# Decoder step: the down projection of the ConvFFN's full groups in five matmuls a block in place of six

## What is computed

```python
def conv_ffn(hn, w_up, w_fconv, w_down, prefix):
    up = hn @ w_up                              # 2048 -> 2 x 5504
    up_c, state = causal_dwconv(up, prefix, w_fconv)
    g, u = jnp.split(up_c, 2, axis=-1)
    return (jax.nn.silu(g) * u) @ w_down, state # 5504 -> 2048
...
ffn, ffn_st = conv_ffn(rms_norm(x, norm_ffn), w_up, w_fconv, w_down, ffn_prefix)
x = x + ffn
```

## Time and profile before

| | us |
|---|---|
| median of three runs | 2513.88 |
| lowest and highest of them | 2513.48, 2515.24 |
| the profiled execution, its own time | 2513.66 |
| span of that execution, first to last instruction | 2512.1 |
| mean granted TensorE clock, share of full speed | 0.995 |

### The profile page before, as it was taken

The page is one execution under the profiler, slowest core; times in us unless marked ns, Lnnn a source line. Parts: engine busy times, 40 slices in busy tenths (PEclk is TensorE's granted clock), DMA queues, the critical chain, the costliest instruction groups (busy, mean ns, idle before and its releaser), DMA issues.

```text
span 2512.1 us, 45839 instructions
## 1 busy us (share of the span) xinstructions
PE 2484.5 (99%) x19827; PEld 2461.3 (98%) x19827; DVE 1214.0 (48%) x2028; ACT 636.3 (25%) x857; POOL 128.7 (5%) x158
## 2 busy tenths in 40 slices
PE   9999999999999999999999999999999999999997
PEld 8999999999999999999999999999999999999996
DVE  6824554547323556553355434554355534544346
ACT  7422222223223352222122211222122211222123
POOL 0010101000111030000000000000000000000004
PEclk9999999999999999999999999999999999999999
DMA  7332323242622332232222222222223222232223
GB/s 286 110 115 84 109 86 107 82 127 62 230 94 85 135 82 85 85 100 86 85 85 90 96 85 85 90 91 89 85 85 97 80 94 83 87 99 85 94 77 117
DMA packets 69722, 252.73 MB, mean 101 GB/s; under 512 B 8504, under 2 KB 12936, under 8 KB 68256
## 3 DMA queue, kind: packets, MB, share of 16 engines
q1 hardware_dynamic: 64144, 224.16, 27.6%
q0 software_dynamic: 5248, 25.71, 3.0%
q10 hardware_dynamic: 144, 0.05, 0.0%
HBM read 240.80 MB, written 9.09 MB: 99 GB/s over the span
## 4 chain that ended last, share of the span: by engine, by line
PE 94%; DVE 3%; DMA 1%; POOL 1%; issue 1%; ACT 0%; SPq 0%; DVEq 0%; POOLq 0%; ACTq 0%
PE ps_out L979 89%; POOL sq_sum L640 1%; DVE x_t L1895 1%; PE ps_out L1035 0%; PE ps_out L1037 0%; PE ps_out L1036 0%; DVE w_lo L1383 0%; DMA out_conv_s<-pe 0%; DVE a_lo L1389 0%; DMA w_raw<-in_wall 0%; PE ps_out L1238 0%; DMA x_t<-in_x 0%; PE ps_b L1044 0%; PE ps_out L1271 0%; DVE x_t L1904 0%
## 5 line engine op out<-in xcount | busy, mean ns | idle before, releaser
L979 PE MATMUL ps_out<-a_hi,w_hi 128*128 128x272 f32 x4704 | 978.2, 290 | 3.2 <-DVE w_lo L1383 3.2
L979 PE MATMUL ps_out<-a_lo,w_hi 128*128 128x272 f32 x4704 | 975.2, 289 | 0.0
L979 PE MATMUL ps_out<-a_hi,w_lo 128*128 128x272 f32 x4704 | 975.0, 289 | 0.0
L979 PEld LDWEIGHTS ps_out<-a_hi,w_hi 128*128 128x128 f32 x4704 | 738.5, 189 | 7.6 <-issue 6.6
L979 PEld LDWEIGHTS ps_out<-a_lo,w_hi 128*128 128x128 f32 x4704 | 738.5, 188 | 0.0
L979 PEld LDWEIGHTS ps_out<-a_hi,w_lo 128*128 128x128 f32 x4704 | 738.1, 188 | 0.0
L662 ACT ACTIVATE w_hi<-w_raw 128x1024 fp32r<-128x1024 f32 x402 | 410.9, 1050 | 695.9 <-PE ps_out L979 679.5
L1383 DVE TENSOR_TENSOR w_lo<-w_raw,w_hi 128x1024 fp32r<-128x1024 f32 x402 | 481.6, 1229 | 133.9 <-ACT w_hi L662 130.0
L1418 DVE TENSOR_TENSOR x_t<-ps_out,x_t 128x544 f32<-128x544 f32 x112 | 81.1, 724 | 414.9 <-PE ps_out L979 402.2
L979 PE MATMUL ps_out<-h_hi,w_hi 128*128 128x272 f32 x1280 | 265.3, 289 | 0.4
L979 PE MATMUL ps_out<-h_lo,w_hi 128*128 128x272 f32 x1280 | 264.9, 288 | 0.0
(11 more groups left out here) (356 smaller groups left out, 1524.4 us busy)
## 6 DMA issues: line engine op xcount, KB each, us to landing
w_raw<-in_wall SPq DMA_DIRECT2D x406, 512.0 KB, 3.8
x_t<-in_x SPq DMA_DIRECT2D x4, 1088.0 KB, 9.3
x_t<-in_x POOLq DMA_DIRECT2D x4, 1088.0 KB, 10.2
kc_t<-in_k_cache POOLq DMA_DIRECT2D x1, 4096.0 KB, 24.0
vc_t<-in_v_cache POOLq DMA_DIRECT2D x1, 4096.0 KB, 13.8
out_y<-x_t SPq DMA_DIRECT2D x7, 544.0 KB, 3.0
rows<-gate_rows POOLq DMA_DIRECT2D x4, 816.0 KB, 7.2
c_smp<-in_c_smp POOLq DMA_DIRECT2D x4, 512.0 KB, 7.7
```

What stands on the lines that cost most here:

```text
L979: ins_ = nc.tensor.matmul(out_bank(o, k)[:, 0:n[1]][:, ::-1], w, a[:, c, m:m + n[1]][:, ::-1], start=first and t == 0, stop=last and t == 2)
```

## The change

The eight chunks' high and low parts, which lay in two tiles of 544 columns a chunk, lie in one tile `h_seg` of 1088 columns a chunk, cut in three segments: the first 272 high columns and the first 92 low ones (`LA`) of the one half, the same of the other half, and the remaining 180 low columns of both halves (`LB`). With the high weight TensorE multiplies the three segments, 364, 364 and 360 columns, into the two banks of the output and one bank of `ps_a`. With the low weight it multiplies the two high parts, 272 columns each, into the first 272 columns of the output's banks (`five`). The waits and the two counts of `half_used` a unit stay where they were. In the banks, the low terms of a half now lie in two places beside the rest, so VectorE's addition to `x_t` becomes three (`add_five`): the `ps_a` bank, the last 92 columns of the output's banks, and the old one, which waits for the second. ScalarE writes the high part in three copies, VectorE the low part in four subtractions. The rest of three chunks keeps the old layout (`plain`).

```diff
--- before.py
+++ after.py
@@ -199,6 +199,12 @@
         kc_t = at("kc_t", R_Y, [P, H, NB, NM])
         h_hi = at("h_hi", R_Y, [P, GRP, T], F32R)
         h_lo = at("h_lo", R_Y + GRP * T * 4, [P, GRP, T], F32R)
+        LA = 92
+        LB = TH - LA
+        h_seg = at("h_seg", R_Y, [P, GRP, 2 * T], F32R)
+        hs_hi = h_seg[:, :, 0:2 * (TH + LA)].rearrange("p c (a t) -> p c a t", a=2)[:, :, :, 0:TH]
+        hs_la = h_seg[:, :, 0:2 * (TH + LA)].rearrange("p c (a t) -> p c a t", a=2)[:, :, :, TH:TH + LA]
+        hs_lb = h_seg[:, :, 2 * (TH + LA):2 * T].rearrange("p c (a t) -> p c a t", a=2)
         l_hi = at("l_hi", R_AH, [P, LDN_UNITS - RING, UB * P], F32R)
         l_lo = at("l_lo", R_AL, [P, LDN_UNITS - RING, UB * P], F32R)
         w_raw = at("w_raw", R_RAW, [P, RING, UB * P])
@@ -903,7 +909,7 @@
             split_hi(Index(U_FFN + 3))
 
 
-            def hidden(u0, j, c, first):
+            def hidden(u0, j, c, first, plain=False):
 
                 if not (first and j == 0):
                     splits(u0 + 4 * j)
@@ -913,8 +919,14 @@
                 nc.scalar.activation(cv[0][:, 0:CEXT - 2], cv[0][:, 0:CEXT - 2], ACT.Silu).then_inc(g_silu, 1)
                 splits(u0 + 4 * j + 2)
                 act.wait_ge(h_prod, (c + 1).value())
-                nc.scalar.activation(h_hi[:, j, 0:SEQ], cv[0][:, 0:SEQ], ACT.Copy).then_inc(h_hi_done, 1)
-                nc.scalar.activation(by_smp(h_hi[:, j, SEQ:T]), smp(cv[0], 2)[:, :, 0:NT], ACT.Copy).then_inc(h_hi_done, 1)
+                if plain:
+                    nc.scalar.activation(h_hi[:, j, 0:SEQ], cv[0][:, 0:SEQ], ACT.Copy).then_inc(h_hi_done, 1)
+                    nc.scalar.activation(by_smp(h_hi[:, j, SEQ:T]), smp(cv[0], 2)[:, :, 0:NT], ACT.Copy).then_inc(h_hi_done, 1)
+                else:
+                    nc.scalar.activation(hs_hi[:, j, 0, :], cv[0][:, 0:TH], ACT.Copy)
+                    nc.scalar.activation(hs_hi[:, j, 1, 0:SEQ - TH], cv[0][:, TH:SEQ], ACT.Copy).then_inc(h_hi_done, 1)
+                    nc.scalar.activation(by_smp(hs_hi[:, j, 1, SEQ - TH:TH]), smp(cv[0], 2)[:, :, 0:NT],
+                                         ACT.Copy).then_inc(h_hi_done, 1)
 
             def group(u0, c0, first=False):
                 for j in range(GRP):
@@ -926,7 +938,7 @@
             for g in range(1, NG):
                 group(Index(U_FFN + g * FU), Index(g * GRP))
             for j in range(REST):
-                hidden(Index(U_LAST), j, Index(NG * GRP + j), False)
+                hidden(Index(U_LAST), j, Index(NG * GRP + j), False, plain=True)
 
             def final_root(n):
                 act.wait_ge(ssq, S_FIN + n + 1)
@@ -1300,25 +1312,43 @@
                     pe.wait_ge(h_lo_done, (c0 + c + 1).times(2).value())
                 return wait
 
+            def five(o, u, chunks, marks, wait=None, late=False):
+
+                s = u.mod(RING)
+                pe.wait_ge(hi_ready, (u + 1).value())
+                pe.wait_ge(lo_ready, (u + 1).value())
+                seg = TH + LA
+                places = [(out_bank(o, 0), 0, seg), (out_bank(o, 1), seg, 2 * seg), (ps_a[:, o.mod(2), :], 2 * seg, 2 * T)]
+                for c in chunks:
+                    if wait is not None:
+                        wait(c)
+                    wh, wl = w_hi[:, s, P * c:P * c + P], w_lo[:, s, P * c:P * c + P]
+                    for n, (bank, a, z) in enumerate(places):
+                        m = nc.tensor.matmul(bank[:, 0:z - a][:, ::-1], wh, h_seg[:, c, a:z][:, ::-1], start=c == 0,
+                                             stop=n == 2 and c == GRP - 1, skip_group_check=True)
+                    if late:
+                        m.then_inc(half_used, 1)
+                    for bank, a, z in places[0:2]:
+                        m = nc.tensor.matmul(bank[:, 0:TH][:, ::-1], wl, h_seg[:, c, a:a + TH][:, ::-1], start=False,
+                                             stop=c == GRP - 1, skip_group_check=True)
+                    if c in marks:
+                        m.then_inc(half_used, 1)
+
             def down2(o, u, wait):
 
                 for m in range(2):
                     free(o + m)
-                    blocks(o + m, u + m, [(b, b, b == 0, False, m == 0 and b == 3) for b in range(GRP - 1)],
-                           h_hi, h_lo, (2, TH), wait if m == 0 else None)
+                    five(o + m, u + m, range(GRP - 1), (3,) if m == 0 else (), wait if m == 0 else None)
                 for m in range(2):
 
-                    blocks(o + m, u + m, [(GRP - 1, GRP - 1, False, True, True)], h_hi, h_lo, (2, TH),
-                           wait if m == 0 else None, late=m == 1)
-
+                    five(o + m, u + m, [GRP - 1], (GRP - 1,), wait if m == 0 else None, late=m == 1)
             def group(u0, o0, c0, first=0):
                 for j in range(first, 2 * GRP):
                     output(o0 + j, u0 + 2 * j, a_hi, a_lo)
                 down2(o0 + 2 * GRP, u0 + 4 * GRP, hidden_waits(c0))
                 for m in range(2, KD):
                     free(o0 + 2 * GRP + m)
-                    blocks(o0 + 2 * GRP + m, u0 + 4 * GRP + m, [(b, b, b == 0, b == GRP - 1, b % 4 == 3) for b in range(GRP)],
-                           h_hi, h_lo, (2, TH))
+                    five(o0 + 2 * GRP + m, u0 + 4 * GRP + m, range(GRP), (3, GRP - 1))
 
             group(Index(U_FFN), Index(O_FFN), Index(0), first=1)
             for g in range(1, NG):
@@ -1416,6 +1446,15 @@
             def add_to_x(o, m):
 
                 tt(halves(x_t[:, m, :]), out_view(o), halves(x_t[:, m, :]), ALU.add).then_inc(evacuated, 1)
+
+            def add_five(o, m):
+
+                x = halves(x_t[:, m, :])
+                own = ps_out[:, 2 * o.mod(2):2 * o.mod(2) + 2, :]
+                rest = ps_a[:, o.mod(2), 0:2 * LB].rearrange("p (a t) -> p a t", a=2)
+                tt(x[:, :, LA:TH], rest, x[:, :, LA:TH], ALU.add)
+                link(tt(x[:, :, 0:LA], own[:, :, TH:TH + LA], x[:, :, 0:LA], ALU.add))
+                tt(x, out_view(o), x, ALU.add).then_inc(evacuated, 1)
 
             def conv3(dst, src, taps):
 
@@ -1846,7 +1885,7 @@
             for e in ext:
                 link(nc.vector.memset(e[:, 0:2], 0.0))
 
-            def hidden(u0, o0, j, c, first):
+            def hidden(u0, o0, j, c, first, plain=False):
 
                 for k in range(2):
                     n = (c.times(2) + k).value()
@@ -1867,9 +1906,18 @@
                 dve.wait_ge(g_silu, (c + 1).value())
                 tt(cv[0][:, 0:CEXT - 2], cv[0][:, 0:CEXT - 2], cv[1][:, 0:CEXT - 2], ALU.mult).then_inc(h_prod, 1)
                 dve.wait_ge(h_hi_done, (c + 1).times(2).value())
-                tt(h_lo[:, j, 0:SEQ], cv[0][:, 0:SEQ], h_hi[:, j, 0:SEQ], ALU.subtract).then_inc(h_lo_done, 1)
-                tt(by_smp(h_lo[:, j, SEQ:T]), smp(cv[0], 2)[:, :, 0:NT], by_smp(h_hi[:, j, SEQ:T]), ALU.subtract)\
-                    .then_inc(h_lo_done, 1)
+                if plain:
+                    tt(h_lo[:, j, 0:SEQ], cv[0][:, 0:SEQ], h_hi[:, j, 0:SEQ], ALU.subtract).then_inc(h_lo_done, 1)
+                    tt(by_smp(h_lo[:, j, SEQ:T]), smp(cv[0], 2)[:, :, 0:NT], by_smp(h_hi[:, j, SEQ:T]), ALU.subtract)\
+                        .then_inc(h_lo_done, 1)
+                else:
+                    tt(hs_la[:, j, :, :], cv[0][:, 0:2 * TH].rearrange("p (a t) -> p a t", a=2)[:, :, 0:LA],
+                       hs_hi[:, j, :, 0:LA], ALU.subtract)
+                    tt(hs_lb[:, j, 0, :], cv[0][:, LA:TH], hs_hi[:, j, 0, LA:TH], ALU.subtract)
+                    tt(hs_lb[:, j, 1, 0:SEQ - TH - LA], cv[0][:, TH + LA:SEQ], hs_hi[:, j, 1, LA:SEQ - TH],
+                       ALU.subtract).then_inc(h_lo_done, 1)
+                    tt(by_smp(hs_lb[:, j, 1, SEQ - TH - LA:LB]), smp(cv[0], 2)[:, :, 0:NT],
+                       by_smp(hs_hi[:, j, 1, SEQ - TH:TH]), ALU.subtract).then_inc(h_lo_done, 1)
 
             def group(u0, o0, c0, first=False):
                 for j in range(GRP):
@@ -1877,13 +1925,13 @@
                 for m in range(KD):
                     splits(u0 + (4 * GRP + m), 1)
                     summed(u0 + (4 * GRP + m))
-                    add_to_x(o0 + (2 * GRP + m), m)
+                    add_five(o0 + (2 * GRP + m), m)
 
             group(Index(U_FFN), Index(O_FFN), Index(0), first=True)
             for g in range(1, NG):
                 group(Index(U_FFN + g * FU), Index(O_FFN + g * FO), Index(g * GRP))
             for j in range(REST):
-                hidden(Index(U_LAST), Index(O_LAST), j, Index(NG * GRP + j), False)
+                hidden(Index(U_LAST), Index(O_LAST), j, Index(NG * GRP + j), False, plain=True)
 
             def final_scale(n):
                 dve.wait_ge(root, S_FIN + n + 1)
```

## The result

| | us |
|---|---|
| before, median of 15 runs | 2514.80 (2511.85 to 2516.21) |
| changed, median of 15 runs | 2520.29 (2517.83 to 2523.76) |
| ratio | 1.0024, 95% interval 1.0017 to 1.0032 |
| changed, the profiled execution, its time and its span | 2520.72, 2519.2 |

The changed kernel is slower by 4 to 8 us, where 3 us less was forecast and the range ended at 2518.5. The page shows what was meant to happen: 640 matmuls fewer than in the earlier trace rows, and the work of VectorE grown by 68 us. But the span grew.

The account below looks back on a forecast made before the run. TensorE's unbroken matmuls were taken to bound the kernel: -7.43 us for fewer matmuls and +4.15 us for the additions gave -3.3 us, stated as 2510.6 us; own range 2508.8 to 2512.6, widened to 2508.5 to 2518.5.

Parts of the forecast that it names:

- What bounds the kernel: ConvFFN: one unbroken stretch of matmuls per group, 287.54 us for 2298, plus one VectorE addition of 0.74 us a group.
- A fixed 11.7 ns for each matmul instruction, whatever its width: Down outputs: one matmul fewer in each of 640 blocks saves 11.7 ns each, 7.49 us in all.
- The ends of that term: Matmul saving: either the fixed part vanishes on three wide matmuls, 22.5 us more saved, or nothing is saved.
- One that grows with the columns (nothing saved): Down matmuls: overhead is a share of the columns, nothing saved, +4.15 us, 2518.0 us; rival's chance 0.05.
- The pieces of 16 columns: Down matmuls: operand fetched in whole 16-column pieces, three more a block, 20 ns, +9.5 us in sum, 2523.4; chance 0.12.
- The three additions: VectorE's addition to x: 1.55 us in place of 0.72, seen once in each of five groups, +4.15 us.
- What stays hidden: ScalarE's extra copies and VectorE's extra subtractions: last low half at most 0.6 us later, under 3.8 us of cover.
- The clock: Longer TensorE stops, some 1.05 us, lower the granted clock: +4.1 us, 2518.0 us; rival's chance 0.05.
- Slower: Whole kernel above 2518.9 us: chance 0.14, from the 16-column pieces (0.12) and 0.02 of the two rivals at 2518.

Follow-up runs that it names:

- noflip: The changed kernel with the five matmuls of a block reading and writing their columns in ascending, not descending, order: 2512.10 us in a single run, 740.2 ns a block.
- la88_noflip: The changed kernel in ascending order with LA = 88 in place of 92, a single run: 740.4 ns a block.
- la96: The changed kernel with LA = 96 in place of 92, all segments on multiples of 16 columns: 2522.25 us against 2514.22 before, ratio 1.0030.
- la94: The changed kernel with LA = 94 in place of 92, segments starting at columns 0, 366 and 732, a single run: 753.4 ns a block.
- dve3: The kernel before with three VectorE operations in place of each one addition of a down output: 2518.20 us, ratio 1.0017.
- before_cover: The kernel before with blocks reordered so that three, not one, cover a group's first addition: 2511.68 us against 2514.06, ratio 0.9991.
- readflip: The changed kernel reading operands in descending order as it does but writing PSUM in ascending order, a single run: 752.1 ns a block on average.
- best_w32: The kernel of noflip_cover with the split weights 32 bytes further on in SBUF: 2519.45 us against 2514.78 before, ratio 1.0018.
- wshift: The changed kernel, descending, with the split weights and all behind them 64 bytes further on in SBUF: 2526.86 us, single run, beside 2516.84 before.
- best_w128: The kernel of noflip_cover with the split weights 128 bytes further on in SBUF: 2512.07 us against 2514.78 before, ratio 0.9989.
- la94_noflip: The changed kernel in ascending order with LA = 94 in place of 92, a single run: 740.0 to 750.0 ns a block, differing by group.
- before_noflip: The kernel before with the matmuls of line 979 reading and writing in ascending order: 2519.52 us against 2514.07, ratio 1.0022.
- zero_h: The changed kernel with the high and low operands of the full groups set to zero: 2523.75 us in a single run.
- psoff: The changed kernel, descending, with the third segment's 360 columns at the end of their PSUM bank, a single run: 289.58 us a group.
- noflip_cover: The changed kernel with its five matmuls ascending and three blocks covering a group's first addition: 2507.11 us against 2514.07 before, ratio 0.9969.

## Why the prediction was wrong

- **What bounds the kernel.** Right. The loss lies in the two places that were named, the matmuls of the down outputs and the one addition on the chain. Nothing else in the stage waits.
- **A fixed 11.7 ns for each matmul instruction, whatever its width.** This is the step that failed. It rested on two widths, 256 and 272 columns, 6% apart, and was carried to 364, and on rows of one order and one placement. One argument for it carried nothing, that the loss doesn't come with a change of weights: the earlier trace rows has as many weight loads as matmuls, 19827 each, so every matmul brings a load whether its weights change or not. Over the 680 ns that 1632 columns stream, a block of six loses 70 ns, one of five 73.3 in the changed kernel, and 60 to 73.4 over all cuts, orders and placements tried. In the best of them (740.0 ns) it is 12.0 ns an instruction, in the changed kernel 14.7. So one instruction less can be worth 10 ns a block, but in the changed kernel that is gone and 3 ns more are lost; why this layout loses them is open. The term was -7.4 us and came out at +2.1 (640 x 3.3 ns).
- **The ends of that term.** "One that grows with the columns (nothing saved)" was taken as the upper end, and its rival got 0.05. The measured 753.3 ns lies 3 ns beyond it. The contradiction that I saw, 0.4622 against 0.4597 ns a column, is a difference of 0.7 ns in a step, less than layout alone moves them (13.3 ns over five steps, noflip): an upper end has to allow for that. It isn't shown that the loss is a share of the columns; noflip and la88_noflip speak against it.
- **The pieces of 16 columns.** Rightly given as the way to slower, with the right sign, a place and a price (20 ns a block, 14.8 measured), but the mechanism has fallen (la96, la94).
- **The three additions.** Right: 1.55 us on VectorE, and 0.81 us more of stop for each group where 0.83 was worked out, 4.05 us in five (dve3 measures 4.0 us by the medians, before_cover takes the stop away).
- **What stays hidden.** Right. No wait for the last chunk's halves appears, and the longer work for it changed nothing.
- **The clock.** It stayed at 1.00 behind the longer stops of the groups, as expected. It fell in the tail, in some executions, at a stop that was there before.
- **The chances.** "Slower" had 0.14 and the range ended 1.8 us short of the median. With the failed term at its upper end the sum would have been 2518.0, on the edge; the term's own uncertainty was set from how well two rows agreed and not from how far they were carried.

What makes the difference is shown as far as this: the order of reading and writing at this cut, and in it the direction of the read (noflip, readflip); where the weights lie against the operand by 32, 64 or 128 bytes (best_w32, wshift, best_w128); something that can change at a stop of TensorE and then holds (la94_noflip, readflip, before_noflip); not the data (zero_h), not this place in PSUM (psoff), not a grid of columns, not the work of VectorE and ScalarE beside it. That weight loads and operand reads meet in SBUF, at some offsets more than at others, fits all of it. But it is argued: no view shows a single collision, and offsets alone aren't enough, since the same ones give different times behind different stops. What would decide it, a block with its weights loaded once, wasn't tried.

## What to carry to other kernels

A step read at two near widths is a point, not a line: before an instruction count is traded for width, the new width, order and placement have to be measured, and a term carried that far needs an end that reaches past zero. Work added to an engine that is half idle is paid in full where its result is the last thing waited for; moving two blocks of independent work behind that place took it off (before_cover, noflip_cover). And where a stage is one unbroken stream of matmuls, the order of the read and the place of the weights are worth a try of a few bytes each: here they moved a block by up to 13 ns and the whole kernel by some 12 us (2507.11 in noflip_cover, 2519.45 in best_w32, measured at different times; by the steps, 0.52 ns for 14448 matmuls at line 991 and 6.7 for 640 blocks, it is 11.8). A single trace isn't enough to tell: the same instructions can run at one step behind one stop and at another behind the next.

## What the runs showed of the hardware

The loss over streaming isn't a property of the matmul alone. At 272 columns it is 11.7 ns with descending order and the old placement, 12.0 ascending (11.7 in one group), 12.2 with the weights shifted by 32 or 64 bytes and 11.7 again at 128. Blocks of five settle on few times in all these runs, 740.0, 746.7, 750.0 or 753.3 ns if neighbours are averaged; these lie multiples of 3.33 ns apart, the time in which eight columns stream (8 x 0.4167). Why is open. At the lower clock level the loss is not seen: two matmuls take 0.45 us where their streaming takes 0.453.

The Trainium skill, page "TensorE: Matmul & The Clock Gate", section "Step-by-step: what each phase is for", has the moving operand and the weights come through two independent read ports of SBUF. The runs don't show ports; but steps that change when, of the operands of these matmuls, the weights alone lie 64 bytes further on (125.03 to 125.55 ns) are not what two streams with nothing to do with each other would give.
